# Two model blocks in one tuned kernel: four edits to the order of its work, and a longer warm-up

## What is computed

```python
# first block, twice
proj = rms_norm(h) @ w_in            # q, k, v, index keys, conv inputs, rz (recurrence inputs), gates
y_a = dsa_attention(...)             # 8 heads, keys chosen by top-k
y_b = short_conv_mixer(...)
y_c = rwkv7_time_mix(...)            # kk = kk * rsqrt(sum over a head of kk*kk); group norm at the end
h = h + sum(sigmoid(gate_g) * (y_g @ w_branch[g]) for g in (a, b, c)) @ w_out
h = h + conv_glu_ffn(rms_norm(h))
# second block, twice
u = rms_norm(h) @ w_in               # two sets of q, k, v, gate
ya = dilated_mixture(qa, ka, va) * silu(za)      # 16 heads, in pairs: 8 steps
yb = diff_attention(qb, kb, vb, lam) * silu(zb)  # 8 heads of two softmaxes: 8 steps
h = h + (sigmoid(ga) * (ya @ w_a) + sigmoid(gb) * (yb @ w_b)) @ w_out
```

## Time and profile before

| | us |
|---|---|
| median of 3 runs | 1680.03 (1679.94 to 1680.36) |
| profiled execution | 1679.88 |
| its span, first to last instruction | 1678.1 |
| PE busy | 1660.4 (99%) |
| PE weight loads busy | 1478.3 (88%) |
| DVE busy | 1196.9 (71%) |
| ACT busy | 964.0 (57%) |

### The profile page before, as it was taken

How to read it: one execution, slowest core, us unless ns; L and a number is a source line. 1 busy time by engine, 2 the same in 40 slices (tenths; PEclk the granted TensorE clock), 3 DMA queues, 4 the chain that set the end, 5 groups by cost and what they waited for, 6 DMA issues and landing times.

```text
span 1678.1 us, 29746 instructions
## 1 busy us (share of the span) xinstructions
PE 1660.4 (99%) x12378; PEld 1478.3 (88%) x12378; DVE 1196.9 (71%) x1676; ACT 964.0 (57%) x1459; POOL 211.7 (13%) x208
## 2 busy tenths in 40 slices
PE   8999999999999999999999999999999999999998
PEld 6999999999998999999999998778888987788887
DVE  7877446798888975538898875767766647667664
ACT  7674424655567564335555555665774556657743
POOL 1764400000001945200000000000000100000000
PEclk9999999999999999999999999999999999999999
DMA  7443522544545424424455454344344453443451
GB/s 266 147 152 119 178 102 101 201 179 176 185 179 184 173 101 142 155 102 175 152 183 199 176 201 176 129 148 174 128 175 177 169 199 135 150 162 141 163 188 51
DMA packets 48197, 268.17 MB, mean 160 GB/s; under 512 B 13568, under 2 KB 14464, under 8 KB 16448
## 3 DMA queue, kind: packets, MB, share of 16 engines
q1 hardware_dynamic: 38160, 263.65, 43.7%
q10 hardware_dynamic: 9136, 1.58, 0.5%
q0 software_dynamic: 768, 1.05, 0.3%
HBM read 264.42 MB, written 1.84 MB: 159 GB/s over the span
## 4 chain that ended last, share of the span: by engine, by line
PE 94%; DVE 3%; ACT 2%; issue 1%; DMA 0%; DVEq 0%; SPq 0%; ACTq 0%
PE bank L1488 12%; PE bank L1489 11%; PE bank L1490 11%; PE bank L2647 11%; PE bank L2649 10%; PE bank L2648 10%; PE bank L1541 8%; PE bank L1543 4%; PE bank L2677 2%; PE bank L2665 1%; DVE w_low L967 1%; PE bank L1937 1%; PE bank L1776 1%; ACT w_high L594 1%; PE bank L1778 1%; PE bank L1777 1%
## 5 line engine op out<-in xcount | busy, mean ns | idle before, releaser
L967 DVE TENSOR_TENSOR w_low<-slab,w_high 128x2048 fp32r<-128x2048 f32 x249 | 579.9, 2338 | 207.0 <-ACT w_high L594 199.7
L594 ACT ACTIVATE w_high<-slab 128x2048 fp32r<-128x2048 f32 x249 | 470.2, 1895 | 139.6 <-PE bank L2649 97.2
L1488 PE MATMUL bank<-act,w_high 128*128 128x256 f32 (+1 forms) x1744 | 503.1, 288 | 5.8 <-DVE act L1101 4.4
L1489 PE MATMUL bank<-act,w_high 128*128 128x256 f32 (+1 forms) x1744 | 493.9, 283 | 0.0
L1490 PE MATMUL bank<-act,w_low 128*128 128x256 f32 (+1 forms) x1744 | 493.7, 283 | 0.0
L1488 PEld LDWEIGHTS bank<-act,w_high 128*128 128x128 f32 (+1 forms) x1744 | 333.4, 191 | 17.1 <-issue 11.2
L1489 PEld LDWEIGHTS bank<-act,w_high 128*128 128x128 f32 (+1 forms) x1744 | 333.7, 191 | 0.9 <-issue 0.5
L1490 PEld LDWEIGHTS bank<-act,w_low 128*128 128x128 f32 (+1 forms) x1744 | 333.7, 191 | 0.1
L2647 PE MATMUL bank<-w_high,act 128*128 128x512 f32 x768 | 305.3, 398 | 0.0
L2649 PE MATMUL bank<-w_low,act 128*128 128x512 f32 x768 | 299.8, 390 | 0.0
L2648 PE MATMUL bank<-w_high,act 128*128 128x512 f32 x768 | 299.1, 389 | 0.0
(11 more groups left out here) (261 smaller groups left out, 1853.8 us busy)
## 6 DMA issues: line engine op xcount, KB each, us to landing
slab<-stream_a SPq DMA_DIRECT2D x143, 1024.0 KB, 4.8
slab<-stream_b SPq DMA_DIRECT2D x104, 1024.0 KB, 4.8
residual<-x_t SPq DMA_DIRECT2D x4, 256.0 KB, 6.0
slab<-stream_a ACTq DMA_DIRECT2D x2, 512.0 KB, 5.6
lora_weights<-lora SPq DMA_DIRECT2D x2, 512.0 KB, 7.7
out_t<-residual SPq DMA_DIRECT2D x4, 256.0 KB, 2.3
d_inverse<-arena POOLq DMA_DIRECT2D x2, 256.0 KB, 3.4
constants<-common SPq DMA_DIRECT2D x1, 384.0 KB, 8.8
```

Of the source, the lines that this page charges most:

```text
L594: line.did(eng.activation(core.wh[u % PARTS][:, 0:SLAB_WIDTH[u]], core.slab[u % SLABS][:, 0:SLAB_WIDTH[u]], ACT.Copy), core.sem("slab_high"))
L967: line.did(line.eng.tensor_tensor(core.wl[u % PARTS][:, 0:SLAB_WIDTH[u]], core.slab[u % SLABS][:, 0:SLAB_WIDTH[u]], core.wh[u % PARTS][:, ...
L1488: eng.matmul(out, wh, xh, start=first, stop=False, skip_group_check=True)
L1489: eng.matmul(out, wh, xl, start=False, stop=False, skip_group_check=True)
```

## The change

Four edits. In `woven` a third way to place `split_next` is added, behind the mid steps and ahead of the unit's rest, and `("gc", 2)` moves to it from `late`. `kk_sum` moves from behind `rz` 5 to behind `rz` 6. The slots of the second block put `qk_turn` first and `pv` behind `scores`, and the slot's rounding behind `qk_turn`. The warm-up has six matmuls in place of three.

```diff
-def woven(units, first, lead, after, mid, last=False, early=(), late=()):
+def woven(units, first, lead, after, mid, last=False, early=(), late=(), behind_mid=()):
...
-        if units[u] not in late:
+        if units[u] not in late and units[u] not in behind_mid:
             steps += split_next
         if units[u] in mid:
             steps += [("begin", u)] + mid[units[u]]
+        if units[u] in behind_mid:
+            steps += split_next
...
-    put(("rz", 5), ("kk_sum", 0))
-    put(("rz", 6), ("kk_root", 0))
+    put(("rz", 6), ("kk_sum", 0), ("kk_root", 0))
...
     return woven(UNITS_A, first, lead_steps(first), after, mid, early=[("br2", 0), ("br2", 1)],
-                 late=[("gc", 2), ("br2", 1)])
+                 late=[("br2", 1)], behind_mid=[("gc", 2)])
...
-            put(UNITS_B[host + n], ROUND_NEXT)
-            for name, lag in (("pv", 3), ("turned" if late else "turn", 2), ("scores", 1), ("combine", 1), ("qk_turn", 0)):
+            for name, lag in (("qk_turn", 0), ("turned" if late else "turn", 2), ("scores", 1), ("pv", 3), ("combine", 1)):
                 if name == "combine":
                     put(UNITS_B[host + n], SPLIT_NEXT)
                 if 0 <= n - lag < 8:
                     put(UNITS_B[host + n], (name, 8 * kind + n - lag))
+                if name == "qk_turn":
+                    put(UNITS_B[host + n], ROUND_NEXT)
...
-    for _ in range(3):
+    for _ in range(6):
         eng.matmul(core.bank[6][:], flat(core, IDLE_)[:, 0:P], flat(core, IDLE_, 2), start=True, stop=True, skip_group_check=True)
```

## The result

The changed kernel takes 1671.79 us (median of 5 runs, 1671.33 to 1671.93), the kernel before 1680.11 us in the same session (1679.94 to 1680.36). The ratio is 0.9947, 95% interval 0.9936 to 0.9959. 1671.9 us was predicted, with a range of 1670.0 to 1676.0. The profiled execution has a span of 1670.1 us, that of before 1678.1.

A forecast was written before the change was run, and what follows sets the result against it. PE, 99% busy, was taken as the bound. 3.5 (`gc` 2, first layer) + 2.5 (second) + 1.4 (head sums) + 0.7 (slots) = 8.1 us off the median 1680.03 gave 1671.9 us, range 1670.0 to 1676.0.

The forecast's parts named there:

- `gc` 2, the first layer: First-block layer one, rounding moved ahead: 2.19 us wait gone, 1.4 from the clock, less 0.1 at a split: 3.5 us.
- the second: Second first-block layer, rounding moved ahead: 2.19 us wait gone plus 0.35 at the split behind: 2.5 us.
- 0.5 us to spare: At `gn` 2: DVE's two subtractions end about 761.3 and 762.0, ahead of PE being ready at 762.46.
- The wait at the split behind it: Second layer, PE's 0.51 us wait for a split at 782.77: shrinks by 0.35 us.
- The slow clock: First layer, 1.2 GHz stretch behind the long wait: does not fall without the wait, 1.4 us, between 0 and 1.7.
- the rival's remark that chance has a part: Rival: slow stretch moves elsewhere instead of going, as only one of two like waits had it; 1673.3 us, chance 0.14.
- Head sums: Keys' head sums behind `rz` 6: two 0.5 us waits and one shape excursion go; 1.4 us both layers, bounds 1.0-1.6.
- ACT's delay: ACT's root, rounding, table load and first exponentials move by up to 1.7 us behind the moved head sums; costed at nothing.
- The slots: Second block's slots, both runs: 0.7 us gained in sum, from 2.0 us gained to 1.5 us lost.
- the pair `scores` to `pv`: First run's slots: 64 rows to 64 columns costs a switch, so 0.12 us less a slot; 0.2 if none.
- `turn`'s lost cover: Second run of slots: `turn` stands first in slots 8 and 9, `scores` little earlier; 0.15 us lost in each layer.
- The warm-up: Program start: three more matmuls of zeros fill idle time, PE then waits at 16.60; costed at nothing, at most 0.4 lost.

## Why the prediction was right, step by step

**`gc` 2, the first layer: 3.5 forecast, 3.9 measured; the second: 2.5 and 3.0.** The mechanism is the one forecast: rounding 746.46, split 748.40, `gn` 2 in one row, no wait. The 0.5 us to spare that the text gave turned out as 757.38 - 757.09 = 0.3 us to the last of two subtractions. Both sizes were low in the main for one reason: a wait costs more than its idle time. Without the 2.19 us PE gained 2.35 + 0.07. The two starts around the wait in the kernel before:

```profile
271.69 0.28 PE L1490 MATMUL bank<-act,w_low 128*128 128x256 f32 x1
274.16 0.36 PE L1488 MATMUL bank<-act,w_high 128*128 128x256 f32 x1 [2.19 <-DVE act L1101]
```

They stand 2.47 us apart. The list counts the idle time from the end of the first of them, but in a row the next one would have started 0.12 us after its start: 2.47 - 0.12 = 2.35. The other 0.07 is the start behind, which comes after 0.19 us in place of 0.12. That this is the weight load, which finds nothing to overlap with, is my reading; no run measured it by itself. The wait at the split behind it was to shrink by 0.35 us; it went altogether, 0.57 us in the second layer with the same overhead.

**The slow clock: 1.4 forecast, 1.5 measured in the pair of profiles.** "Without the wait I expect it not to fall" held, and so did the rival's remark that chance has a part. With the wait, the slow stretch came at 275 us in the profiles of the kernel before and of that with 6 zeros, and did not come in that with `gc` 2 undone, behind the same 2.19 us. Executions of the three kernels that have the long waits spread over 2.0 to 2.7 us where there are 9 or more in a session, with mean clocks that fall as the time grows. The changed kernel's lie within 0.6, but they are only five, and five of the kernel before once lay within 0.4; the kernel with `combine` ahead of the split, which has other waits of up to 1.6 us in the second block, spread over 1.7 us in 11. So that the slow stretch belongs to this one wait alone isn't shown. Of the edit's gain 3.0 us in each layer are shown at full clock (the steps of the run that undid it), and some 0.9 more come or not with the slow stretch, which costs 1.5 but hides the next wait of 0.57. The Trainium skill, "TensorE: Matmul & The Clock Gate", says in Part 1 that the moment at which the clock rises under steady matmuls varies from run to run by half a microsecond. No run here shows that figure; what the profiles show is that after the same wait the clock may fall or not.

**Head sums: 1.4 forecast, 1.55 measured,** inside the bounds. ACT's delay was hidden, as costed.

**The slots: 0.7 forecast, under 0.1 measured (from +2.0 to -1.5 allowed).** This is the term that was mis-sized. In the first run all was as worked out: 0.11 to 0.12 us in a middle slot, and the pair `scores` to `pv` costs a change of shape (0.31 us between their starts, as from a unit to `pv` in the earlier trace rows). In the second run the text gave `turn`'s lost cover 0.15 us a layer; the run lost 0.4 to 0.5, of which slots 3 and 8 are 0.3. The text had looked at slot 9, where the earlier trace rows show a wait already, and taken `pv` alone as its cover. The round trip from `scores` to `combine` has 0.3 to 0.4 us to spare in the middle slots of that run and none in slots 3 and 8, and the text never added it up.

**The warm-up: 0 forecast, 0 measured.** The second slab stands 10.95 us behind ACT's first step with 3 zeros and with 6. The +0.50 us in the pair of profiles, 17.10 where the prediction looked for 16.6, is the first transfer, 6.16 against 5.67 us, which no step of the prediction carried.

**The sum** of 8.1 us met the measured 8.3 (8.0 in the pair of profiles) because the terms' errors cancel: `gc` 2 and the clock 0.9 too low, head sums 0.15 too low, slots 0.65 too high, and the start 0.5 us later by chance. The mechanisms of `gc` 2 and the head sums were right; that the total came within 0.2 us is luck.

## What to carry to other kernels

Price a wait of TensorE by what follows it too: the first matmul behind it, and a clock that may fall. On an in-order engine look at what an instruction that is "in the way" stands in front of; if the one behind it must wait for another engine anyway, it is filling, and once it is moved the engine does both in turn, the wait and the work (here 1.93 and 2.28 us, and 8.16 us for a slot). A reordering that pays in one loop can lose in its twin: give each loop its own order, count changes of array shape (here 0.11 to 0.15 us each), and put the start of the longest round trip early and its consumer late.

## What was not expected of the hardware

- The same idle time is followed by the lower clock in one execution and not in another. 2.19 us of waiting in the first layer were followed by 3.4 us at 1.2 GHz in two profiles and by none in a third; in the second layer it never came in a profile.
- The tail pays too: the last two matmuls, behind 1.07 us of idle time, took 1.22 us in some profiles and 0.70 in others, a difference of 0.5 us in the time that no edit made.
- One change of shape more or less in a slot, between full weights and a half set or between the two kinds of half set, is worth 0.11 to 0.15 us of PE's time, with no wait of PE in the record. The Trainium skill, "TensorE: Matmul & The Clock Gate", says in Part 3 that a weight load overlaps matmuls in flight only when it goes to another group of rows. The page of the changed kernel doesn't agree, with loads busy 1477.8 us and matmuls 1658.8 of 1670.1, nearly all on all rows. The loads that do stand idle in the slots are those behind a change of shape: 1.3 us in 8 times ahead of L2679 and 2.0 in 6 ahead of L2711, in the list of the weight loads above.
